# The last 64 tokens leave the dense expert sum: their picked rows of v come by indirect loads and VectorE sums them

## The reference, cut to what matters

```python
idx = jnp.take_along_axis(cand_i, pos, axis=-1)      # 128 experts a token, of 128 x 128
g = jax.nn.softmax(top_s, axis=-1)                   # their gates
u_sel = jnp.take(u_tab, idx, axis=0)
h = jnp.einsum('bthkd,btd->bthk', u_sel, xb)
a = (jax.nn.gelu(h.astype(jnp.float32)) * g).astype(xb.dtype)
return jnp.einsum('bthk,bthkd->btd', a, jnp.take(v_tab, idx, axis=0))
```

## Time and profile before

| | |
|---|---|
| median of 3 runs (lowest, highest) | 1757.11 us (1756.68, 1757.22) |
| profiled execution, its span | 1757.71 us, 1755.1 us |
| PE, PEld busy in the span | 1728.4 us (98%), 1523.5 us (87%) |
| DVE, ACT, POOL busy | 1003.2, 945.6, 1133.0 us |
| granted TensorE clock | 0.998 of full speed |
| u stage, first half; second half; v stage | about 299 to 484; 484 to 719; 719 to 1071 us of the span |

### The profile page before, as it was taken

One profiled execution on the slowest core, in us unless ns is written; L12 is line 12 of the kernel. 1 busy time (PEld: TensorE's weight loads), 2 busy tenths in 40 slices (PEclk: granted clock), 3 DMA queues, 4 the chain that ended last, 5 costly groups with the idle time before them and its releaser, 6 DMA issues.

```text
span 1755.1 us, 33424 instructions
## 1 busy us (share of the span) xinstructions
PE 1728.4 (98%) x12454; PEld 1523.5 (87%) x12454; DVE 1003.2 (57%) x1927; ACT 945.6 (54%) x1414; POOL 1133.0 (65%) x506
## 2 busy tenths in 40 slices
PE   8999999999999999999999999999999999999998
PEld 6888899999999999888888887988888989978887
DVE  5224333992478888544444446465555985665555
ACT  5468454446544444455444456666657762346565
POOL 6966776887888888655555556755566463555553
PEclk9999999999999999999999999999999999999999
DMA  8543443665544444566667763455544521245552
GB/s 303 195 157 130 159 173 141 184 184 181 175 148 141 140 143 143 168 192 192 192 207 253 242 191 108 169 216 192 191 150 138 178 63 52 66 156 194 190 190 83
DMA packets 68094, 292.57 MB, mean 167 GB/s; under 512 B 13184, under 2 KB 13712, under 8 KB 50464
## 3 DMA queue, kind: packets, MB, share of 16 engines
q1 hardware_dynamic: 67808, 291.12, 50.8%
q0 software_dynamic: 48, 0.08, 0.0%
q10 hardware_dynamic: 144, 0.07, 0.0%
HBM read 289.14 MB, written 1.05 MB: 165 GB/s over the span
## 4 chain that ended last, share of the span: by engine, by line
PE 80%; POOL 9%; issue 5%; ACT 2%; DVE 2%; DMA 1%; POOLq 0%; DVEq 0%; SPq 0%; ACTq 0%
PE bank L1060 8%; POOL rows_lo L2983 7%; PE bank L876 7%; PE bank L1081 6%; PE bank L938 6%; PE bank L941 6%; PE bank L935 6%; PE bank L1196 4%; PE bank L1064 4%; PE bank L882 4%; PE bank L618 4%; PE bank L624 4%; PE bank L619 4%; PE bank L908 3%; PE bank L647 1%
## 5 line engine op out<-in xcount | busy, mean ns | idle before, releaser
L2968 POOL TENSOR_TENSOR unit_lo<-unit_raw,unit_hi 128x2048 fp32r<-128x2048 f32 (+1 forms) x86 | 332.9, 3886 | 132.4 <-ACT unit_hi L1649 119.6
L2983 POOL TENSOR_TENSOR rows_lo<-rows_raw,rows_hi 128x1024 fp32r<-128x1024 f32 x128 | 309.6, 2420 | 84.8 <-ACT rows_hi L1769 46.0
L3010 POOL TENSOR_TENSOR a_lo<-table,a_hi 128x256 fp32r<-128x256 f32 x128 | 178.7, 1396 | 159.7 <-ACT a_hi L1848 159.6
L2567 DVE TENSOR_TENSOR rows_lo<-rows_raw,rows_hi 128x1024 fp32r<-128x1024 f32 x128 | 161.8, 1264 | 185.5 <-ACT rows_hi L1844 185.5
L1844 ACT ACTIVATE rows_hi<-rows_raw 128x1024 fp32r<-128x1024 f32 x128 | 135.6, 1060 | 168.4 <-PE bank L941 168.4
L3040 POOL TENSOR_TENSOR up_lo<-up_raw,up_hi 128x2048 fp32r<-128x2048 f32 x22 | 111.2, 5054 | 156.5 <-ACT up_hi L1920 126.9
L1649 ACT ACTIVATE unit_hi<-unit_raw 128x2048 fp32r<-128x2048 f32 x70 | 134.0, 1918 | 65.4 <-PE bank L624 36.9
L1060 PE MATMUL bank<-x_lo_hi,up_hi 128*128 128x512 f32 x640 | 159.8, 392 | 0.4 <-DVE acc L2660 0.4
L882 PE MATMUL bank<-x_lo_hi,rows_lo 128*128 128x256 f32 x1024 | 143.2, 282 | 0.5 <-POOL rows_lo L2983 0.5
L882 PEld LDWEIGHTS bank<-x_lo_hi,rows_lo 128*128 128x128 f32 x1024 | 135.7, 190 | 6.6 <-POOL rows_lo L2983 0.9
L938 PE MATMUL bank<-rows_hi,a_lo 128*128 128x512 f32 x512 | 138.5, 391 | 0.8 <-POOL a_lo L3010 0.8
(11 more groups left out here) (491 smaller groups left out, 3929.2 us busy)
## 6 DMA issues: line engine op xcount, KB each, us to landing
unit_raw<-in_ring SPq DMA_DIRECT2D x70, 1024.0 KB, 5.0
rows_raw<-in_u SPq DMA_DIRECT2D x128, 512.0 KB, 3.6
rows_raw<-in_v SPq DMA_DIRECT2D x128, 512.0 KB, 3.6
up_raw<-in_up SPq DMA_DIRECT2D x44, 1024.0 KB, 5.2
down_raw<-in_down SPq DMA_DIRECT2D x22, 1024.0 KB, 4.9
unit_raw<-in_ring SPq DMA_DIRECT2D x20, 256.0 KB, 3.6
const<-in_const SPq DMA_DIRECT2D x1, 1792.0 KB, 15.0
X<-in_x SPq DMA_DIRECT2D x2, 512.0 KB, 5.7
```

The costliest lines, as they stand in the source:

```text
L2567: V.tensor_tensor(rows_lo[q][:, :], rows_raw[q][:, :], rows_hi_f[q % 2], ALU.subtract).then_inc(S("v_lo_ready"), 1)
L2968: return nc.gpsimd.tensor_tensor(unit_lo[SLOT_OF[n]][:, w], unit_raw[SLOT_OF[n]][:, w], hi, ALU.subtract)
L2983: nc.gpsimd.tensor_tensor(rows_lo[q][:, :], rows_raw[q][:, :], rows_hi_f[q % 2], ALU.subtract).then_inc(S("u_lo_ready"), 1)
L3010: nc.gpsimd.tensor_tensor(a_lo[q % 2][:, :], table[:, i * ROWS_RING + q, :], a_hi_f[q % 2], ALU.subtract).then_inc(S("a_lo_ready"), 1)
```

## The change

For the last 64 tokens (`SPARSE`), 192 remain dense (`DENSE`).

*Gates.* 48 groups instead of 64: 6 in each round of 8 tiles, none at places 6 and 7.

*TensorE in the v stage.* a_hi has 192 columns. For the second token half the stationary operand is one buffer of 128 columns: the remainders of 64 tokens (made by POOL) beside the high parts of the same 64 tokens (a second, small copy by ACT). Its matmuls give both products at once, in two halves of the PSUM rows, which DVE adds at the end.

*The last 64 tokens.* DVE works out row numbers (128 x key 1 + key 2) and places. Each of 128 partitions holds one token and half of its 128 picks, so 64 picks a partition. SP writes these tokens' gelu(h) to DRAM during the u stage, 16 transfers of 8 tiles in runs of 64 numbers. In the v stage POOL issues 64 indirect loads of one number a partition (`fetch_hidden`) and 64 of one row of v a partition, 512 KB each (`fetch_rows`, ring of 3). DVE multiplies by the gates in batches of 16 and sums row by row into PSUM (`selected_sum`), 64 instructions of 128 x 1024. The v loop on DVE and POOL is written out.

Some semaphores are merged to free their numbers (const, biases, sd_ready); those edits wait for the same or slightly more loads.

```diff
+SPARSE = 64
+DENSE = SEQ - SPARSE
+PARTS = P // SPARSE
+PICKED = SLOTS // PARTS
+GATHER_RING = 3
+    BATCH = 16
+    SUM_TILE = [20 + n * 103 // PICKED for n in range(PICKED)]
+    FETCH_TILE = [4 + n * 13 // BATCH for n in range(BATCH)] + [SUM_TILE[n - BATCH] + 1 for n in range(BATCH, PICKED)]
...
             for q in range(ROWS_RING):
-                gate_group(q, q)
+                if q < ROUND_GROUPS:
+                    gate_group(q, q)
                 hidden(HALF_TILES + q, q, False, wide=True)
...
-                pe.wait_ge(S("a_hi_ready"), t + 1)
+                first_hi, first_lo, both = a_hi[q % 2][:, 0:P], a_lo[q % 2][:, 0:P], a_lo[q % 2][:, P:2 * P]
+                pe.wait_ge(S("a_hi_ready"), t * 2 + 2)
                 for c, h in places:
-                    mm(out_bank(c, h), tokens(a_hi[q % 2], c), half_rows(rows_hi[q % 2], h), start=first, stop=False, skip_group_check=True)
+                    if c == 0:
+                        mm(out_bank(0, h), first_hi, half_rows(rows_hi[q % 2], h), start=first, stop=False, skip_group_check=True)
                 pe.wait_ge(S("a_lo_ready"), t + 1)
                 for c, h in places:
-                    mm(out_bank(c, h), tokens(a_lo[q % 2], c), half_rows(rows_hi[q % 2], h), start=False, stop=False, skip_group_check=True)
+                    if c == 0:
+                        mm(out_bank(0, h), first_lo, half_rows(rows_hi[q % 2], h), start=False, stop=False, skip_group_check=True)
+                    else:
+                        mm(out_bank(1, h), both, half_rows(rows_hi[q % 2], h), start=first, stop=False, skip_group_check=True)
                 pe.wait_ge(S("v_lo_ready"), t + 1)
                 for c, h in places:
-                    m = mm(out_bank(c, h), tokens(a_hi[q % 2], c), half_rows(rows_lo[q], h), start=False, stop=last, skip_group_check=True)
+                    m = mm(out_bank(c, h), both if c else first_hi, half_rows(rows_lo[q], h), start=False, stop=last, skip_group_check=True)
...
+                def keep_hidden(at_):
+                    sp.dma_start(kept[bass.ds(at_, ROWS_RING)].rearrange("e p t -> p e t"), table[:, bass.ds(at_, ROWS_RING), DENSE:]).then_inc(S("hidden_kept"), 16)
...
-                    A(a_hi[q % 2][:, :], table[:, t, :], ACT.Copy).then_inc(S("a_hi_ready"), 1)
+                    A(a_hi[q % 2][:, :], table[:, t, 0:DENSE], ACT.Copy).then_inc(S("a_hi_ready"), 1)
+                    A(a_lo[q % 2][:, DENSE:], table[:, t, P:DENSE], ACT.Copy).then_inc(S("a_hi_ready"), 1)
...
+            def selected_sum(n):
+                ve.wait_ge(S(f"gathered{n % GATHER_RING}"), 16 * (n // GATHER_RING + 1))
+                row = gathered[n % GATHER_RING][:, :]
+                if n % BATCH == 0:
+                    ve.wait_ge(S("hidden_gathered"), 16 * (n + BATCH))
+                    w = slice(n, n + BATCH)
+                    step(V.tensor_tensor(picked_h[:, w], picked_h[:, w], picked_gate[:, w], ALU.mult))
...
+                    ve.wait_ge(S("sparse_used"), n)
+                    V.scalar_tensor_tensor(sparse_sum, row, picked_h[:, n:n + 1], sparse_sum, ALU.mult, ALU.add).then_inc(S("sparse_used"), 1)
+            for t in range(N_KEYS):
...
+                V.tensor_tensor(rows_lo[q][:, :], rows_raw[q][:, :], rows_hi_f[q % 2], ALU.subtract).then_inc(S("v_lo_ready"), 1)
+                for n in range(PICKED):
+                    if SUM_TILE[n] == t:
+                        selected_sum(n)
+                if t == N_KEYS - 2:
+                    for part in range(PARTS):
+                        ve.wait_ge(S("sparse_used"), PICKED + part)
+                        x = X[P - SPARSE:P, 1, :]
+                        V.tensor_tensor(x, sparse_sum[part * SPARSE:(part + 1) * SPARSE, :], x, ALU.add).then_inc(S("sparse_used"), 1)
...
+                    x = X[0:P - SPARSE, 1, w]
+                    step(V.tensor_tensor(x, o[P - SPARSE:P, :], x, ALU.add))
+                    V.tensor_tensor(x, o[0:P - SPARSE, :], x, ALU.add).then_inc(S("experts_added"), 1)
...
+            def fetch_rows(n):
+                if n >= GATHER_RING:
+                    g.wait_ge(S("sparse_used"), n - GATHER_RING + 1)
+                nc.gpsimd.indirect_dma_start(gathered[n % GATHER_RING][:, :], None, d_v.rearrange("a b d -> (a b) d"),
+                                             bass.IndirectOffsetOnAxis(ap=picked_row[:, n:n + 1], axis=0)).then_inc(S(f"gathered{n % GATHER_RING}"), 16)
+            rows_tile = [SUM_TILE[0] - 6] * GATHER_RING + [t + 1 for t in SUM_TILE[0:PICKED - GATHER_RING]]
+            for t in range(N_KEYS):
+                activations_lo(t)
...
+                for n in range(PICKED):
+                    if FETCH_TILE[n] == t:
+                        fetch_hidden(n)
+                    if rows_tile[n] == t:
+                        fetch_rows(n)
```

More of the change, by code:

```diff
@@ L1478, in _ @@
                     sp.dma_start(rows_raw[q][:, :], d_v[q]).then_inc(S(f"u{q}_loaded"), 16)
+                for n in (2, 1):
+                    sp.wait_ge(S("hidden_in_table"), N_KEYS - HALF_TILES - ROWS_RING * (n - 1))
+                    keep_hidden(N_KEYS - ROWS_RING * n)
                 def v_rounds(start, stop):
@@ L2530, in hidden_sum, with gates_into_table @@
                 V.tensor_tensor(o, o, hidden_lo[:, :], ALU.add).then_inc(S("hidden_added"), 1)
-            def gates_into_table(n, q, first=False, second=False, last=False):
-                if not first:
-                    hidden_sum(n - 1, (q - 1) % ROWS_RING)
-                ve.wait_ge(S("gates_filled"), n + 1)
+            def gates_into_table(n, g, q, last=False):
+                ve.wait_ge(S("gates_filled"), g + 1)
                 if not last:
-                    one_hots(n + 1)
-                if first or second:
+                    one_hots(g + 1)
+                if isinstance(n, int) and n < 2:
                     ve.wait_ge(S("hidden_used"), HALF_TILES)
@@ L2543, in gates_into_table, with second_half_round @@
                     ve.wait_ge(S("hidden_in_table"), n - 1)
-                h = table[:, :, bass.ds(n * 4, 4)]
+                h = table[:, :, bass.ds(g * 4, 4)]
                 V.tensor_tensor(h, PS[6 + q % 2][:, :].rearrange("p (q n) -> p n q", q=4), h, ALU.mult).then_inc(S("gates_applied"), 1)
-                ve.wait_ge(S("gates_applied"), n + 1)
+                ve.wait_ge(S("gates_applied"), g + 1)
+            def second_half_round(i, first=False, last=False):
+                for q in range(ROWS_RING):
+                    n = i * ROWS_RING + q
+                    if not (first and q == 0):
+                        hidden_sum(n - 1, (q - 1) % ROWS_RING)
+                    if q < ROUND_GROUPS:
+                        gates_into_table(n, i * ROUND_GROUPS + q, q, last and q == ROUND_GROUPS - 1)
             one_hots(0)
@@ L2551, in _ @@
             step.sync()
-            for q in range(ROWS_RING):
-                gates_into_table(q, q, first=q == 0, second=q == 1)
-            with ve.Fori(1, GROUPS // ROWS_RING - 1) as i:
-                for q in range(ROWS_RING):
-                    gates_into_table(i * ROWS_RING + q, q)
-            for q in range(ROWS_RING):
-                gates_into_table(GROUPS - ROWS_RING + q, q, last=q == ROWS_RING - 1)
+            second_half_round(0, first=True)
+            with ve.Fori(1, HALF_ROUND - 1) as i:
+                second_half_round(i)
+            second_half_round(HALF_ROUND - 1, last=True)
             hidden_sum(N_KEYS - HALF_TILES - 1, ROWS_RING - 1)
```

147 lines of the change are left out of this document (94 added, 53 removed).

## The result

| | before | after |
|---|---|---|
| median of 4 runs (lowest, highest), us | 1756.89 (1756.65, 1757.22) | 1769.38 (1769.30, 1772.96) |
| profiled execution, its span, us | 1757.71, 1755.1 | 1772.96, 1771.1 |
| granted TensorE clock | 0.998 | 0.992 |

The ratio is 1.0076, 95% interval [1.0058, 1.0093]: 12.5 us or 0.76% slower, where 17 us less was forecast. The time lies in the given range, on the other side of no change.

A forecast was written before the change was run, and what follows sets the result against it. PE, busy 98%, bounds the kernel, a chain close behind in the v stage. -13.6 - 25.7 + 8.5 + 4 + 8 + 1.5 = -17.3 us on 1757.7: median 1740 us, own range 1727 to 1752, full range 1712 to 1785.

The forecast's parts named there:

- The gates: 16 of 64 gate groups go, each costing PE 0.85 us: -13.6 us.
- The chain: V stage: ACT, DVE's rows_lo, POOL's a_lo, then 8 matmuls set 2.52 us a tile, above PE's 2.275: -25.7 us.
- The price of a load: POOL's time for one indirect load in the v stage: 1.1 us, near ends 0.71 and 1.29, far end 2.4.
- The pairs: V stage, two loads on POOL in 48 tiles: 2.3 us in a 1.92 us gap, 0.4 us late, +8.5 us.
- the prediction's own way over five tiles: Two steps of two tiles at 5.04 + 0.4 and one tile at 2.275: 13.16 us, 2.63 a tile.
- the lock takes the second load: Rival, v stage: second load waits for rows_lo's end, a_lo 1.3 us late, +36 instead of +8.5, 1768 us; chance 0.18.
- the rival's 1.1: In the lock rival the second load waits until rows_lo ends at S+2.59 and itself ends at S+3.7.
- The batches: V stage, DVE's sum waits for hidden values at tiles 45, 71, 97: 4.5, 2 and 2 us, +8 (0 to 20).
- The burst behind tile 14: V stage: four loads behind tile 14 and three pairs in the first 16 tiles, +4 us (1 to 8).
- the 9.5 us from which they would decide: Rival, row loads land late: beyond 9.5 us each sum stops DVE; at 12 us, +50, 1790 us; chance 0.12.
- a full house: Rival, DMA engines fill in the v stage: 106 MB at 313 GB/s takes 339 us, total 1742 to 1756; chance 0.10.

The follow-up runs named there:

- the one-input run: Changed kernel with DVE's rows_lo subtracting a PSUM bank instead of rows_hi (result then wrong), all loads kept: 1729.13 us, ratio 0.9845.
- the early batches: Changed kernel with the hidden values of batches 2 to 4 fetched three tiles earlier: 1745.96 us, ratio 0.9942.
- single edits: Changed kernel with only the row loads and sums (1723.55 us), or with only the hidden loads (1725.16 us).
- the slack for a_lo: TensorE needs a_lo two matmuls later: on the changed kernel 1779.31 us; with loads also respread (fewer pairs, early batches) 1732.27 us.

## Why the prediction was wrong

*The gates.* Forecast -13.6, measured -13.5. Right.

*The chain.* 2.52 us a tile without pairs: measured 2.52 without loads and in tiles 17 to 20, and 2.54 with single row loads in tiles 100 to 119. The last 8 tiles took 2.80 against 2.93 before. Forecast -25.7; without the loads the v stage took 326.6 us instead of 351.8, -25.2. Right.

*The price of a load.* Bounded by 0.71 and 1.29 us, taken at 1.1; it is 0.96. The gaps were too small: a pair was given 0.1 us of them, and the trace has 0.15 us before the first load and 0.30 us before the second. Unheld, a pair takes 2.4 us, so the two errors nearly cancel. The sum of 1.28 us on DVE against 1.21 forecast made no difference that shows.

*The pairs: the step that failed.* "One load is free. Two, in 48 tiles, take 2.3 us with gaps: 0.4 us late" let both loads run beside rows_lo, although the same text had just read from the earlier trace rows that POOL stands still while DVE reads two operands from SBUF, and applied it to a_lo. Price and gaps do not explain the miss: two unheld loads with the measured gaps take 2.4 us, 0.5 late, and by the prediction's own way over five tiles that is 2.66 us a tile, +11 us. The real ones take 0.96 + 0.30 + 1.23 or more and throw the next load too. The step gave +8.5 us; the three dense stretches measured +26.8. The rival for this, "the lock takes the second load", had 0.18, with 2.99 us a tile and 1768 us; measured were 2.88 to 2.90 us a tile. With the measured 0.82 us from the end of rows_lo to the end of the held load, in place of the rival's 1.1, its own working gives 2.87. Its condition (a load over 0.84 us) was met by the value taken, 1.1, and by the next row, 1.29, though not by the nearest, 0.71. The only argument against it was that a load might read its numbers in another way, for which no row spoke; it should have been the forecast. The mechanism is shown twice: by which loads are held in the changed kernel (45 of the 49 that begin under rows_lo, none of the 79 others), and by the one-input run, in which only an operand of DVE changed and the loads lost their tail. Its share of the 40 us of that run is an estimate.

The Trainium skill's rule (SBUF — State Buffer, "Who interferes with whom") that a DVE instruction with two SBUF inputs holds off GpSimd work that reads SBUF is what these runs show, and for indirect loads too. The same section says that a `tensor_tensor` was not seen to stall GpSimd's DMAs; here indirect loads, which read their row numbers from SBUF, went from 0.96 to as much as 1.99 us beside one.

*The batches.* Forecast +8 (4.5, 2 and 2), measured +17.1 (8.0, 2.6 and 6.5). The row load was taken to land in 3.6 us; in the changed kernel rows_raw of v takes 4.7 us and the gathered rows 6.1. The clock was not in the sum: behind two of the three stops the matmuls ran at the lower level, 2.7 and 1.7 us lost. That leaves 12.7 us of standstill against the 8 forecast. Of the 23 us that the early batches gave back, 15 lay in the tiles of the stops.

*The burst behind tile 14.* Forecast +4 for the first 16 tiles, measured 3.8 + 6.0: the four loads keep POOL 5.2 us (745.82 to 751.00, one of them held), PE waits 3.4 us for a_lo and goes on at the lower level. Of the 3.8 us in tiles 0 to 14, 0.6 are there without any load.

*The other rivals.* Row loads landed 6.1 us after issue, under the 9.5 us from which they would decide. The DMA engines were not full: 313 GB/s for a full house, scaled from 197 GB/s at 0.63, is refuted by 377 at 0.99; busy share does not scale with bytes from a half-loaded stretch. The Trainium skill (DMA: Bandwidth & Descriptors, "Specifications") gives about 358 GB/s to a core, half of the 716 GB/s of a stack that two cores share; the one core in use here passed it by 5% (377 GB/s).

By the rival's price for the pairs the sum would have been 1768 us for the profiled execution, 1767 for the median; that this nearly hits the median of 1769.4 is in part luck, since its pairs are dearer than measured and its batches and burst cheaper.

## What to carry to other kernels

- A rule read from a row ("POOL stands still while DVE reads two SBUF operands") should be taken to hold for every instruction that the change puts on that engine until a row shows otherwise; here it held for indirect loads. Give the exception the small chance, not the rule.
- Where a load fits a gap of its engine, count the gaps, not the work: one per tile was free, the second fell into the next hold and pushed the one after it. Costs of single edits (5 and 7 us) did not predict both (51 us).
- Values that go through a queue behind large loads need the landing time of the loaded kernel, and a stop can cost TensorE's clock besides (in the changed kernel those in which PE stood for 3.4, 4.9 and 5.1 us did, those of 1.5 us and less did not). Take the stops away first: here the slack for a_lo paid only then.

## What was not expected of the hardware

- An indirect load of 128 numbers and one of 128 rows of 4 KB cost GpSimd the same, 0.96 us, with 0.30 us between two of them and 0.15 us behind a_lo. Begun under a DVE subtraction with two SBUF inputs, a load ended 0.81 to 0.83 us after that subtraction (45 loads); begun before it (by as little as 0.05 us), a load kept its 0.96 us and ran beside it. The same subtraction with one input from PSUM was as long (1.22 us) and held nothing (81 loads began under it).
- The waits for the hidden values of three batches came to 11.1 us even without a row load in POOL's queue; a load of 128 single numbers landed 3.9 us after its issue in the median.
- The core moved 369 and 377 GB/s for 233 us, at DMA shares of 0.97 and 0.99.
